# The low half of each weight chunk in two GpSimd subtractions instead of one

## What is computed

```python
for l in range(DEPTH):                                # DEPTH = 2
    mod = c_act @ w_ada[l] + b_ada[l]                 # six vectors of 1024
    h = rms_norm(x, norm1_g[l]) * (1.0 + sc1) + sh1
    proj = h @ w_in[l]                                # attention, index, scan and gate inputs
    ...                                               # top-k attention, state-space scan
    mixed = (sigmoid(ga) * o_attn + sigmoid(gm) * o_ssm) @ w_out[l]
    x = x + g1 * mixed
    h = rms_norm(x, norm2_g[l]) * (1.0 + sc2) + sh2
    u = causal_dwconv(h @ w_up[l], ffn_conv_w[l], ffn_conv_b[l])
    val, gate = jnp.split(u, 2, axis=-1)
    x = x + g2 * ((jax.nn.silu(gate) * val) @ w_down[l])
# second block, one layer: x + mixer(x), then x + square(relu(h @ w_up)) @ w_down
```

## Time and profile before

| | us |
|---|---|
| median of 3 runs | 1947.29 |
| lowest and highest | 1946.86 to 1948.07 |
| the profiled execution | 1950.46 |
| span of the profiled execution | 1948.8 |

### The profile page before, as it was taken

One profiled execution on the slowest core, in us unless ns is written; L12 is line 12 of the kernel. 1 busy time (PEld: TensorE's weight loads), 2 busy tenths in 40 slices (PEclk: granted clock), 3 DMA queues, 4 the chain that ended last, 5 costly groups with the idle time before them and its releaser, 6 DMA issues.

```text
span 1948.8 us, 33455 instructions
## 1 busy us (share of the span) xinstructions
PE 1725.1 (89%) x13290; PEld 1660.3 (85%) x13290; DVE 1005.3 (52%) x1772; ACT 863.5 (44%) x1411; POOL 1165.8 (60%) x476
## 2 busy tenths in 40 slices
PE   8978998979888999778999888888999895769999
PEld 8978988869888999778988778887999894669999
DVE  3457666456325886557666536424882247334400
ACT  2244444544335663244444454334664442324532
POOL 1346954545365889456865454455888683036886
PEclk8788999989899999888999998899999998578999
DMA  7334743436343558444754355444665652024664
GB/s 261 101 115 152 251 139 130 141 130 225 109 143 126 184 196 286 132 120 135 246 175 137 119 163 163 153 129 119 183 185 179 209 174 87 1 80 137 184 184 131
DMA packets 85513, 302.71 MB, mean 155 GB/s; under 512 B 9840, under 2 KB 12528, under 8 KB 85104
## 3 DMA queue, kind: packets, MB, share of 16 engines
q1 hardware_dynamic: 85360, 300.59, 48.3%
HBM read 299.50 MB, written 1.05 MB: 154 GB/s over the span
## 4 chain that ended last, share of the span: by engine, by line
PE 71%; DVE 15%; ACT 4%; issue 4%; DVEq 3%; DMA 1%; POOL 1%; SPq 0%; ACTq 0%; POOLq 0%
PE gemm_bank L1426 58%; PE turn_bank L1533 2%; DVE ada_acc L735 2%; ACT w_hi L404 2%; PE turn_bank L1503 1%; DVE conv L735 1%; PE outp_bank L1521 1%; PE score_bank L1426 1%; PE score_bank L1503 1%; DMA ada_w<-in_w_ada 1%; POOL w_lo L386 1%; DVE rstd_row L755 1%; DVE idx_score L735 1%; DVE probs L922 1%; PE outp_bank L1568 1%
## 5 line engine op out<-in xcount | busy, mean ns | idle before, releaser
L386 POOL TENSOR_TENSOR w_lo<-w_raw,w_hi 128x1024 fp32r<-128x1024 f32 x472 | 1165.6, 2476 | 771.4 <-ACT w_hi L404 770.9
L404 ACT ACTIVATE w_hi<-w_raw 128x1024 fp32r<-128x1024 f32 x472 | 492.3, 1046 | 767.2 <-PE gemm_bank L1426 738.0
L1426 PE MATMUL gemm_bank<-h_hi,w_hi 128*128 128x256 f32 x2112 | 617.8, 293 | 79.2 <-DVE h_lo L735 28.9
L1426 PE MATMUL gemm_bank<-h_lo,w_hi 128*128 128x256 f32 x2112 | 609.2, 288 | 0.0
L1426 PE MATMUL gemm_bank<-h_hi,w_lo 128*128 128x256 f32 x2112 | 608.6, 288 | 0.0
L1426 PEld LDWEIGHTS gemm_bank<-h_hi,w_hi 128*128 128x128 f32 x2112 | 417.8, 198 | 88.2 <-DVE h_lo L735 30.1
L1426 PEld LDWEIGHTS gemm_bank<-h_lo,w_hi 128*128 128x128 f32 x2112 | 417.8, 198 | 0.1
L1426 PEld LDWEIGHTS gemm_bank<-h_hi,w_lo 128*128 128x128 f32 x2112 | 417.2, 198 | 0.0
L1426 PE MATMUL gemm_bank<-w_hi,h_hi 128*128 128x256 f32 (+2 forms) x704 | 207.2, 294 | 18.4 <-DVE h_lo L735 8.0
L735 DVE SCALAR_TENSOR_TENSOR conv<-gemm_bank,params_sb,conv 128x255 f32<-128x255 f32 (+1 forms) x320 | 139.5, 477 | 140.7 <-ACT conv L567 69.8
L1426 PE MATMUL gemm_bank<-w_lo,h_hi 128*128 128x256 f32 (+2 forms) x704 | 202.7, 288 | 0.0
(11 more groups left out here) (276 smaller groups left out, 2407.4 us busy)
## 6 DMA issues: line engine op xcount, KB each, us to landing
w_raw<-in_stream SPq DMA_DIRECT2D x458, 512.0 KB, 3.6
ada_w<-in_w_ada SPq DMA_DIRECT2D x80, 512.0 KB, 4.7
ada_first<-in_w_ada SPq DMA_DIRECT2D x16, 512.0 KB, 10.5
w_raw<-in_stream SPq DMA_DIRECT2D x8, 256.0 KB, 2.7
alibi_sb<-in_alibi SPq DMA_DIRECT2D x1, 1920.0 KB, 7.2
rows_sb<-in_rows SPq DMA_DIRECT2D x1, 1536.0 KB, 10.5
residual<-in_x_t SPq DMA_DIRECT2D x1, 1024.0 KB, 7.4
out_x<-residual SPq DMA_DIRECT2D x4, 256.0 KB, 4.4
```

The source lines that it names most:

```text
L386: nc.gpsimd.tensor_tensor(w_lo[:, s, 0:n], w_raw[:, s, 0:n], w_hi[:, s, 0:n].bitcast(f32), ALU.subtract).then_inc(lo_ready, 1)
L404: A(w_hi[:, s, 0:n], w_raw[:, s, 0:n], ACT.Copy).then_inc(hi_ready, 1)
L1426: ins = M(o, a, b, start=first and i == 0, stop=last and i == len(passes) - 1, skip_group_check=True)
```

## The change

In POOL's list the one subtraction of a chunk becomes two, each over half of the columns, one after the other. The waits stay in front of the first, and the signal lo_ready is given by the second. With n = 1024 the halves have 512 words for each partition, with 512, 416 and 536 they have 256, 208 and 268. The bytes read and written are the same.

```diff
                 pool.wait_ge(hi_ready, g + 1)
                 if g >= RING:
                     pool.wait_ge(chunk_done, g - RING + 1)
-                nc.gpsimd.tensor_tensor(w_lo[:, s, 0:n], w_raw[:, s, 0:n], w_hi[:, s, 0:n].bitcast(f32),
-                                        ALU.subtract).then_inc(lo_ready, 1)
+                for i in range(2):
+                    e = slice(i * n // 2, (i + 1) * n // 2)
+                    ins = nc.gpsimd.tensor_tensor(w_lo[:, s, e], w_raw[:, s, e], w_hi[:, s, e].bitcast(f32), ALU.subtract)
+                ins.then_inc(lo_ready, 1)
```

## The result

The changed kernel takes 1930.31 us (median of 4 runs, 1927.62 to 1932.84), the kernel before 1947.68 us beside it (4 runs, 1946.86 to 1949.45): ratio 0.9915, 95% interval 0.9897 to 0.9934, so 17.4 us less. The execution profiled after took 1927.62 us, with a span of 1926.0.

A forecast was written before the change was run, and what follows sets the result against it. The chain was 71% PE and 15% DVE, with DVE waiting on POOL's port lock. Gains of 26.3 us, less 4 for second paths, plus 2.8 for the clock, made -25 us: 1923 us, range 1908 to 1936.

The forecast's parts named there:

- The lock, and that a half lets DVE in: Shared SBUF ports: DVE waits out POOL's running instruction; arriving in its first half, it enters after 1.29 us instead of 2.40.
- rival B: POOL's second half keeps the lock ahead of waiting DVE, so no wait shortens: 1950 us, chance 0.09.
- 0.15 us more per chunk, hidden in 0.48 us: POOL's second instruction adds 0.15 us per chunk, 71 us in all, covered by its idle time of 0.48 us per 2.88.
- Rival C: POOL becomes the bound in the three long PE-bound stretches, making the kernel slower: 1965 us, chance 0.07.
- idx_score, 8.8 us and 2.8 for the clock: Index scores, once per layer: four DVE waits shortened by 1.1 us each, twice 4.4; half of PE's clock loss comes back.
- The scan, 4.4 us: Scan of each layer: z_gate and the drain behind a blocked ada_acc gain 1.1 us each, in both layers.
- The attention, 3.3 us: Attention: three blocked ada_acc operations on the chain, two in layer 0 and one in layer 1, gain 3.3 us together.
- The softplus, 0: Softplus: one DVE wait of 1.6 us shortens, but second halves catch the next steps: 0, or 0.3 us lost.
- The down projection of layer 0: a gain of 2.1 us: Layer 0's down projection: DVE waits give 3.9 us, less 1.8 for 12 chunks where POOL is saturated.
- The norms of the last block: 5.5 us: Last block's q and k norms: eight halved DVE waits give 7 us, one operation gets a new wait: 5.5 left.
- The 4 us for second paths: Whole kernel: 4 us taken off the gains, an assumed one in six, because whatever is next late can cut a saving.
- rival A: Gains mostly swallowed by second halves catching the next DVE operation or another path close behind: about 1941 us, chance 0.14.

The follow-up runs named there:

- the three positions of the cut: Each chunk's subtraction of the kernel before cut in two: at the half (1930.31 us), 64 words from the end (1936.57 us), or after the first 64 (1927.79 us).
- the second profile: The changed kernel with halves everywhere, run and profiled again against the kernel before: 1930.65 us, ratio 0.9907.

## Why the prediction was right, and where it was too large

1923 us was forecast and 1930.31 measured, inside the range and on the right side: 17 us of gain instead of 24 on the medians. That the total came out this near is in part luck: two steps below failed, and one cost isn't in the sum. By its own steps:

- **The lock, and that a half lets DVE in.** Right. Against rival B speak the four idx_score waits, f_lo at 1364 ns, and the three positions of the cut. But B wasn't empty: with quarters, five operations saw pieces take the lock one after another. The row on which I excluded it (739.79, a queued instruction of 2.4 us that let DVE in) holds for long pieces. The Trainium skill ("SBUF — State Buffer", Who interferes with whom) says that issue order decides who blocks: the traces with whole, half and third pieces show a queued piece letting DVE in at nearly every boundary, those with quarters show it not doing so at five.
- **0.15 us more per chunk, hidden in 0.48 us.** Right: 0.14 where nothing is in the way, and the up projection kept its 130 us. Rival C is excluded for halves. The total of POOL was put at 50 to 80 us and is 95: the two halves each can wait for DVE, which the sum left out (those of 512 words have a mean of 1379 ns, against 1270 for each half of the 2.54).
- **idx_score, 8.8 us and 2.8 for the clock.** Right: 4.07 us in each layer by the distance, and the stage shrank by 5.2, so that about 1.1 lies behind it, where the forecast had the clock (the mean granted clock in the stage of layer 0 went from 0.83 to 0.93 of full speed): 10.4 for a forecast of 11.6 (one of the two layers gave 3.8 in the second profile).
- **The scan, 4.4 us.** Right: 1.88 in each layer, 3.8.
- **The attention, 3.3 us.** Right. Although the stages move by 3 us with no edit, all three pieces show in distances between neighbouring chunks. From chunk 89 to 91 it is 9.65 us before and 8.73 after, and the same from 275 to 277 in layer 1: 0.9 each. From chunk 95 to 96 it is 6.35 us in all three profiles with whole chunks, and 4.84 to 5.24 in the six with halves there: 1.1 to 1.5. In all 2.9 to 3.3.
- **h_lo, 2.2 us.** 0.8 of 1.1 in each layer, 1.6.
- **The softplus, 0.** Right, and for the reason given: 0.2 us from conv to conv.
- **The down projection of layer 0: a gain of 2.1 us.** This step failed. It took 1.8 us on POOL off a gain of 3.9 on DVE. POOL's extra lasted for 23 chunks and not 12 (67.6 us for 63.9), and that delays the transfers of the last ada tiles, so that what DVE saved was spent in waiting for them: the last ada_acc comes later and not earlier, by 1.6 us in the mean (65.0 of three profiles with halves there, 63.4 of six with whole chunks), which single profiles blur (64.1 to 66.5 and 62.0 to 65.0). Some 4 us of difference to the forecast.
- **The norms of the last block: 5.5 us.** This failed too. Of eight waits halved only those of the q norm stayed, until ACT's root took them back; 0.4 to 0.7 us are left at the end of the k norm, and the next output projection starts 0.6 to 0.9 us later than with whole chunks. What takes the last of it wasn't found. Some 6 us of difference.
- **A term that the sum lacks: Q, K, V beside the scan.** With halves everywhere these stages of the two layers are 1.5 to 3.1 us longer together (three profiles). The forecast allowed for an operation without a wait getting one in the last block alone.
- **The 4 us for second paths.** Such paths exist, but they weren't spread evenly: two places gave nothing, the others nearly all.

Added up with the measured terms: 10.4 + 3.8 + 2.9 to 3.3 + 1.6 - 1.6 - 0.6 to 0.9 = 16.2 to 16.9 us, and 13.1 to 15.4 with the cost in Q, K, V. The medians differ by 17.4 (13 to 20 by the interval); the rest lies in stages that move by themselves, and stays open. In a word: rival A was true of two of the seven places. For both, the row to read had been there: for the first the chain over POOL and SP up to 760, for the second who makes DVE's next input.

## What to carry to other kernels

A subtraction on GpSimd that is off the critical path can still set the time, through VectorE operations that wait for the whole of it; the wait hides inside their duration, so compare the durations of one shape. Cutting the GpSimd instruction shortens these waits, but cut only where the chain is on VectorE, follow each saving to the next thing that is late (a root on ScalarE, a transfer behind GpSimd's signal), and don't cut so small, in a long row without a gap, that VectorE is passed over. Profile one kernel twice before explaining ten microseconds of its span.

## What the runs showed that was not expected

- With pieces of 0.73 us back to back a VectorE operation that takes 0.19 us alone took 15.68 us, and 14.03 in a second execution; the other four places repeated too. With pieces of 0.93, 1.29 and 2.41 us no operation was passed over by two pieces.
- An operation that comes within about 0.1 us of the end of a piece can miss that end and wait for the next piece: ada_acc of 2.41 and 2.44 us in two profiles with halves (0.08 and 0.09 us ahead of the end), of 3.49 us with whole chunks at 197.84 (0.04 us).
- The same kernel's span differed by 13.4 us between two executions: 3.6 before the first chunk, 6.5 in the two attention stages, 1.9 in the down projection, with all DVE operations but those of ada_acc of the same length. The time at the lower granted clock (1.2 GHz) was 297.7 us in the first and 277.3 in the second, and 287.5 in the first profile after.
